# A three-network kernel: the feed-forwards' high weight tiles meet both input parts in one 512-column matmul

## The chip, the cores and the metric

One Trainium2 chip, one of its cores. The metric is the device time of one execution in microseconds (us). TensorE (PE) does the matmuls, VectorE (DVE) and ScalarE (ACT) the elementwise work, GpSimd (POOL) a few sums, SyncE (SP) issues the weight loads.

## The reference

Three networks run one after the other on 256 tokens of width 1024: two layers of feed-forward, attention mixer, feed-forward; two layers of feed-forward, convolution or stick-breaking attention, feed-forward; then two layers of attention and an expert lookup. The eight feed-forwards are what the change touches. Each computes

```python
def _rmsnorm(x, g):
    y = x32 * lax.rsqrt(jnp.mean(x32 * x32, axis=-1, keepdims=True) + RMS_EPS)
    return y * g
def _swiglu(x, w_gate, w_up, w_down):
    return (jax.nn.silu(x @ w_gate) * (x @ w_up)) @ w_down
x = x + 0.5 * _swiglu(_rmsnorm(x, g), w_gate, w_up, w_down)   # D_FF = 2816
```

## The kernel before

Everything lies transposed: a tile has 128 features as partitions and the 256 tokens as columns (T = 256), so x is 8 such tiles (DC = 8) and the hidden layer 22 (FC = 22). Matmuls are in fp32r, and to keep fp32 accuracy every operand is split into a high part (rounded) and a low part (the rest). One product of a 128x128 weight tile with a 128x256 input tile is then three matmuls, in `product`: high weights by high input (L655), high weights by low input (L656), low weights by high input (L657). The two input parts of a tile lie next to each other in memory (`h[:, c, 0]` and `h[:, c, 1]`, 256 columns each).

Weights come as slabs of 1 MB (128 x 2048). SyncE loads them into a ring of four (RING = 4). For each slab ScalarE makes the high part (`round_slab`, L1427, one of three buffers), VectorE the low part in place (`rest_slab`, L1916), and TensorE takes a slab when its low part is there (`take`). The order on each engine is the order in which the code is written; engines meet at semaphores, and an instruction that waits holds everything behind it on its engine.

A feed-forward is 33 slabs. The first 22, one for each hidden tile f, hold gate and up weights: 16 products, into the two banks of one of four bank pairs in PSUM (the accumulator memory). The other 11 (r) hold the down weights of two hidden tiles each: again 16 products, into all eight banks. The norm is applied late. The slabs multiply x times the gain, and the factor 1/rms of each token (`rstd`) is multiplied in when a bank pair is read (L2015). At the start TensorE runs slabs 0 and 1 interleaved and then the sums of squares (L726, L727); from them VectorE makes the mean (L1937), ScalarE the root (L1451) and VectorE the reciprocal (L1939). In the fifth feed-forward, the folded one, this chain is longer (`two_roots`, L2338 to L2343, with two roots on ScalarE, L1495 and L1496), since the final norm of the first network is worked into it. After that VectorE and ScalarE go in ticks, one for each slab. A tick of VectorE:

```python
        for tick in range(FC + 2):
            if tick < FC and not (fold and tick == 1):
                self.rest_slab()
...
            if tick == 0 and not fold:
                self.inverse_root(v.rstd, k.sum_bank[:, 0:T], 1, D)
```

followed by the low part of a hidden tile (L2001), gate times up (L2008), and the read of the bank pair with `rstd` (L2015). In tick f `rest_slab` handles slab f + 2.

## Time and profile before

| | |
|---|---|
| time of three runs | 4002.98 us median (3999.48 to 4004.27) |
| span of the profiled execution, first to last instruction | 4004.4 us |
| PE busy | 3909.7 us, 98% of the span, 34150 matmuls |
| DVE busy | 2736.3 us, 68% |
| ACT busy | 1987.8 us, 50% |
| mean granted clock of TensorE | 0.991 |

The span is what the profile has of the profiled execution's own time; nothing around it is given separately. It lies 1.4 us above the median of the runs and 0.1 us above the longest of them. Matmuls are pipelined: one of 256 columns is shown with 276 ns, but the next starts long before it ends, so rates are read from starts, not from durations. A busy share says that an engine had work in flight, not that it ran at its peak.

### The profile page before, as it was taken

The numbers are of one execution on the slowest core, as the hardware profiler recorded it, in microseconds if no ns is written. First come the engines' busy times: TensorE is split into PE (matmuls) and PEld (weight loads), VectorE is DVE, ScalarE is ACT, GpSimd is POOL, SyncE is SP. The second block draws the span as 40 slices with busy tenths as digits, with TensorE's granted clock in tenths as the row PEclk, the third lists the DMA queues.
The fourth block names the chain that finished last, engine by engine and source line by source line (L and its number), as shares of the span: only waits on it lengthen the run. The fifth ranks groups of instructions, "written<-read, shape, count | busy, mean of one in ns | idle before, by whom it ended". The sixth has DMA issues, their size and how long they took to land.

```text
span 4004.4 us, 78708 instructions
## 1 busy us (share of the span) xinstructions
PE 3909.7 (98%) x34150; PEld 3793.3 (95%) x34150; DVE 2736.3 (68%) x4071; ACT 1987.8 (50%) x2620; POOL 212.2 (5%) x277
## 2 busy tenths in 40 slices
PE   8999999999999999999999999999999999999999
PEld 8979999889998999999997999999998899999999
DVE  6566665666655656567555799956756699974855
ACT  5445444454544545465435545754444544764443
POOL 0011000110002000010023000000000000000000
PEclk9999999999999999999998999999999999999999
DMA  6534555345555455534550455456654455455754
GB/s 237 192 115 151 192 190 190 133 148 195 181 194 182 160 199 184 195 133 173 191 204 34 159 194 181 177 199 233 229 196 153 158 177 193 175 182 202 265 199 158
DMA packets 114791, 720.78 MB, mean 180 GB/s; under 512 B 13328, under 2 KB 13664, under 8 KB 32784
## 3 DMA queue, kind: packets, MB, share of 16 engines
q1 hardware_dynamic: 90144, 652.25, 45.9%
q10 hardware_dynamic: 19200, 37.01, 2.5%
q0 software_dynamic: 5104, 26.49, 1.9%
q8 instruction: 270, 4.42, 0.4%
q14 instruction: 73, 0.60, 0.0%
HBM read 692.48 MB, written 23.22 MB: 179 GB/s over the span
## 4 chain that ended last, share of the span: by engine, by line
PE 87%; DVE 7%; ACT 4%; issue 1%; POOL 0%; DMA 0%; ACTq 0%; DVEq 0%; POOLq 0%
PE psum L655 26%; PE psum L657 26%; PE psum L656 26%; PE psum L1408 3%; DVE slab_low L1916 2%; ACT slab_high L1427 2%; DVE h_parts L2219 1%; PE psum L1065 1%; PE psum L1048 1%; PE psum L875 1%; PE psum L1078 1%; ACT room L1670 1%; DVE room L2248 0%; DVE room L2253 0%; PE psum L1349 0%
## 5 line engine op out<-in xcount | busy, mean ns | idle before, releaser
L1916 DVE TENSOR_TENSOR slab_low<-slab,slab_high 128x2048 fp32r<-128x2048 f32 x622 | 1423.2, 2289 | 738.8 <-ACT slab_high L1427 736.6
L655 PE MATMUL psum<-h_parts,slab_high 128*128 128x256 f32 x5632 | 1578.2, 280 | 28.9 <-DVE h_parts L2219 18.6
L1427 ACT ACTIVATE slab_high<-slab 128x2048 fp32r<-128x2048 f32 x622 | 1189.3, 1912 | 785.4 <-PE psum L657 721.1
L656 PE MATMUL psum<-h_parts,slab_high 128*128 128x256 f32 x5632 | 1556.5, 276 | 0.0
L657 PE MATMUL psum<-h_parts,slab_low 128*128 128x256 f32 x5632 | 1556.1, 276 | 0.0
L655 PEld LDWEIGHTS psum<-h_parts,slab_high 128*128 128x128 f32 x5632 | 1063.5, 189 | 48.8 <-issue 24.0
L655 PE MATMUL psum<-hidden_parts,slab_high 128*128 128x256 f32 x3840 | 1063.5, 277 | 11.4 <-DVE hidden_parts L2166 4.8
L656 PEld LDWEIGHTS psum<-h_parts,slab_high 128*128 128x128 f32 x5632 | 1063.5, 189 | 2.4 <-issue 2.2
L657 PEld LDWEIGHTS psum<-h_parts,slab_low 128*128 128x128 f32 x5632 | 1062.8, 189 | 0.0
L656 PE MATMUL psum<-hidden_parts,slab_high 128*128 128x256 f32 x3840 | 1058.0, 276 | 0.0
L657 PE MATMUL psum<-hidden_parts,slab_low 128*128 128x256 f32 x3840 | 1058.0, 276 | 0.0
L655 PEld LDWEIGHTS psum<-hidden_parts,slab_high 128*128 128x128 f32 x3840 | 722.0, 188 | 21.6 <-issue 12.9
L656 PEld LDWEIGHTS psum<-hidden_parts,slab_high 128*128 128x128 f32 x3840 | 722.2, 188 | 0.0
L657 PEld LDWEIGHTS psum<-hidden_parts,slab_low 128*128 128x128 f32 x3840 | 722.0, 188 | 0.0
L1889 ACT ACTIVATE hidden_parts<-room 128x512 fp32r<-128x512 f32 x128 | 80.9, 632 | 303.7 <-PE psum L657 294.7
L1880 ACT ACTIVATE room<-psum 128x512 f32<-128x512 f32 x128 | 76.5, 598 | 283.1 <-PE psum L657 283.1
L2598 DVE TENSOR_TENSOR hidden_parts<-room,hidden_parts 128x512 fp32r<-128x512 f32 x128 | 88.2, 690 | 135.1 <-ACT hidden_parts L1889 134.9
L2015 DVE TENSOR_TENSOR room<-psum,room 128x512 f32<-128x512 f32 x176 | 121.3, 689 | 62.8 <-PE psum L657 61.7
L2569 DVE TENSOR_SCALAR room<-consts,room 128x128 f32<-128x128 f32 x512 | 136.4, 339 | 0.0
L1408 PE MATMUL psum<-room 128*128 128x128 f32 x1024 | 124.5, 275 | 0.0
L1670 ACT ACTIVATE room<-room 128x128 f32<-128x128 f32 (+1 forms) x160 | 71.4, 448 | 105.6 <-DVE room L2253 78.6
L1408 PEld LDWEIGHTS psum<-room 128*128 128x128 f32 x1024 | 119.4, 191 | 0.0
(346 smaller groups left out, 3326.0 us busy)
## 6 DMA issues: line engine op xcount, KB each, us to landing
slab<-in_up SPq DMA_DIRECT2D x176, 1024.0 KB, 4.8
slab<-in_keys_up SPq DMA_DIRECT2D x128, 1024.0 KB, 4.8
slab<-in_keys_down SPq DMA_DIRECT2D x128, 1024.0 KB, 4.8
slab<-in_down SPq DMA_DIRECT2D x88, 1024.0 KB, 4.8
slab<-in_w_in SPq DMA_DIRECT2D x16, 1024.0 KB, 4.8
slab<-in_wq SPq DMA_DIRECT2D x16, 1024.0 KB, 4.8
peer_gates<-room ACTq DMA_DIRECT2D x64, 256.0 KB, 2.3
room<-peer_gates ACTq DMA_DIRECT2D x64, 256.0 KB, 5.4
```

What stands on the lines that cost most here:

```text
L655: nc.tensor.matmul(out, lhs[0], rhs[0], start=first, stop=False, **options)
L656: nc.tensor.matmul(out, lhs[0], rhs[1], start=False, stop=False, **options)
L657: return nc.tensor.matmul(out, lhs[1], rhs[0], start=False, stop=last, **options)
L1408: mm = nc.tensor.matmul(bank[:, t, :], v.firsts[:, b % 2, t, :], v.seconds[b % 2][:, t, :], start=True, stop=True)
L1427: nc.scalar.activation(k.high[m % PARTS][:, 0:width], k.slabs[m % RING][:, 0:width], ACT.Copy).then_inc(k.rounded.up())
L1670: ex = nc.scalar.activation(row, row, ACT.Exp, bias=small[:, e:e + 1], accum_out=small[:, 4 + e:5 + e])
L1880: nc.scalar.activation(v.hidden[:, at:at + 2, :], k.banks[4 + r % 2].rearrange("p (e t) -> p e t", e=2), ACT.Gelu_apprx_tanh).then_inc(k.a ...
L1889: nc.scalar.activation(k.hidden[:, at:at + 2, 0, :], v.hidden[:, place:place + 2, :], ACT.Copy).then_inc(k.hidden_rounded.up())
L1916: nc.vector.tensor_tensor(k.low[m % RING][:, 0:width], k.slabs[m % RING][:, 0:width], k.high[m % PARTS][:, 0:width], ALU.subtract).then_in ...
L2015: nc.vector.tensor_tensor(both, k.bank_pairs[(f + k.first_pair) % 4][:, :, 0:T], v.rstd.unsqueeze(1).to_broadcast([P, 2, T]), ALU.mult).th ...
L2569: hot = nc.vector.tensor_scalar(v.seconds[b % 2][:, t, :], iota, v.slots[:, 1, t0 + t:t0 + t + 1], v.slots[:, 2, t0 + t:t0 + t + 1], ALU.i ...
L2598: nc.vector.tensor_tensor(k.hidden[:, at:at + 2, 1, :], v.hidden[:, place:place + 2, :], k.hidden[:, at:at + 2, 0, :], ALU.subtract).then_ ...
```

## The change

In the feed-forwards a product is now two matmuls: the high weights meet both input parts as one 512-column operand, which fills a whole bank, and the low weights add high input to the first half of it. The sum of both halves is taken later. For a gate/up slab ScalarE copies the second halves out of PSUM into a new buffer `second`, VectorE adds them to the first halves (`halves_added`), and the multiplication by `rstd` now reads the sum from memory. The first nine down slabs (WHOLE = 9) go the same way; VectorE adds their second halves to x (four instructions), while the last two down slabs keep the three-matmul product and write into the first halves alone. In the first place of a tick ScalarE now copies, and rounds the slab after that; the order of the rest of the tick changes too, and in the start of a feed-forward the roots now stand ahead of the first tick. The core of the diff:

```diff
+WHOLE = FC // 2 - 2
...
+    def product_apart(self, bank, lhs, both, first, last, **options):
+        nc = self.k.nc
+        nc.tensor.matmul(bank, lhs[0], both.rearrange("p a t -> p (a t)"), start=first, stop=False, **options)
+        return nc.tensor.matmul(bank[:, 0:T], lhs[1], both[:, 0], start=False, stop=last, **options)
...
# TensorE.ffn
-                nc.tensor.wait_ge(k.up_scaled.sem, k.up_scaled.at(f - 3))
+                nc.tensor.wait_ge(k.halves_added.sem, k.halves_added.at(f - 3))
...
-            if r == FC // 2 - 1:
-                nc.tensor.wait_ge(k.hidden_ready.sem, k.hidden_ready.at(FC))
+            if r >= WHOLE:
+                last = r == FC // 2 - 1
+                nc.tensor.wait_ge(k.hidden_ready.sem, k.hidden_ready.at(2 * r + 2))
                 for j, e, c in itertools.product(range(DC // 2), range(2), range(2)):
+                    if e == 0 and c == 0 and (last and j < 2 or not last and j == 2):
+                        nc.tensor.wait_ge(k.second_taken.sem, k.second_taken.at(3 + j if last else 2))
...
# ScalarE.ffn
+        else:
+            self.round_slab()
+            self.root(v.rstd)
         for tick in range(FC + 2):
-            if (2 if fold else 0) <= tick < FC:
+            if tick < FC:
+                f = tick
+                nc.scalar.wait_ge(k.slab_done.sem, k.slab_done.at(f + 1))
+                if f >= 2:
+                    nc.scalar.wait_ge(k.halves_added.sem, k.halves_added.at(f - 1))
+                nc.scalar.activation(v.second[:, f % 2], k.bank_pairs[(f + k.first_pair) % 4][:, :, T:2 * T], ACT.Copy).then_inc(k.second_copied.up())
                 self.round_slab()
-            if tick == 0 and not fold:
-                self.root(v.rstd)
...
-        for r in range(FC // 2):
+        for r in range(1, FC // 2):
             self.round_slab()
# VectorE.ffn
+        else:
+            self.inverse_root(v.rstd, k.sum_bank[:, 0:T], 1, D)
         for tick in range(FC + 2):
-            if tick < FC and not (fold and tick == 1):
+            both = v.both[:, tick % 2]
+            if tick < FC:
+                f = tick
+                nc.vector.wait_ge(k.second_copied.sem, k.second_copied.at(f + 1))
+                if f >= 2:
+                    nc.vector.wait_ge(k.multiplied.sem, k.multiplied.at(f - 1))
+                nc.vector.tensor_tensor(both, k.bank_pairs[(f + k.first_pair) % 4][:, :, 0:T], v.second[:, f % 2], ALU.add).then_inc(k.halves_added.up())
                 self.rest_slab()
-            if tick == 0 and not fold:
-                self.inverse_root(v.rstd, k.sum_bank[:, 0:T], 1, D)
...
+            if tick < FC:
+                nc.vector.wait_ge(k.halves_added.sem, k.halves_added.at(f + 1))
+                nc.vector.tensor_tensor(both, both, v.rstd.unsqueeze(1).to_broadcast([P, 2, T]), ALU.mult).then_inc(k.up_scaled.up())
...
-        for r in range(FC // 2 - 1):
+        for r in range(2, FC // 2):
             self.rest_slab()
+        nc.vector.wait_ge(k.slab_done.sem, k.slab_done.at(FC + WHOLE))
+        for n, j in enumerate((3, 2, 0, 1)):
+            halves = k.x[:, 2 * j:2 * j + 2, :]
+            if n >= 2:
+                nc.vector.wait_ge(k.pair_free.sem, k.pair_free.at(j + 1))
+            nc.vector.scalar_tensor_tensor(out=halves, in0=k.bank_pairs[j][:, :, T:2 * T], scalar=0.5, in1=halves,
+                                           op0=ALU.mult, op1=ALU.add).then_inc(k.second_taken.up())
+        nc.vector.wait_ge(k.second_taken.sem, k.second_taken.at(4))
+        self.rest_slab()
         self.owed = True
```

VectorE at the start of the first feed-forward, before. `slab_low_55` is the low part of slab 2, the third slab; L1937 and L1939 are the mean and the reciprocal, L2015 the read of the first bank pair.

```order
L2219 SCALAR_TENSOR_TENSOR h_parts<-x,vectors,h_parts 128x256 [waits h_rounded] x2
L1916 TENSOR_TENSOR slab_low_55<-slab_51,slab_high_59 128x2048 [waits slab_rounded]
L1937 TENSOR_SCALAR room<-psum 128x256 [waits squares_summed]
L1939 RECIPROCAL room<-room 128x256 [waits root_ready]
L2015 TENSOR_TENSOR room<-psum,room 128x512 [waits slab_done,dve_step]
```

The same place in the changed kernel (L1935 is `rest_slab`, L1956 the mean, L1958 the reciprocal, L2009 the sum of the two halves, L2023 the multiplication by `rstd`):

```order
L2247 SCALAR_TENSOR_TENSOR h_parts<-x,vectors,h_parts 128x256 [waits h_rounded] x2
L1956 TENSOR_SCALAR room<-psum 128x256 [waits squares_summed]
L1958 RECIPROCAL room<-room 128x256 [waits root_ready]
L2009 TENSOR_TENSOR room<-psum,room 128x512 [waits second_copied,dve_step]
L1935 TENSOR_TENSOR slab_low_55<-slab_51,slab_high_59 128x2048 [waits slab_rounded]
L2018 MEMSET room 1x16
L2023 TENSOR_TENSOR room<-room 128x512 [waits halves_added]
```

The low part of slab 2 stood ahead of the mean and now stands behind the mean, the reciprocal and the sum of the first halves. TensorE at the same place in the changed kernel (L736 and L737 are the sums of squares, then slab 2 begins):

```order
L736 MATMUL psum<-room,consts 128x256 [waits pool_move,squares_added]
L737 MATMUL psum<-room,consts 128x256
L666 MATMUL psum<-h_parts,slab_high_59 128x512 [waits small_load,slab_rest]
L667 MATMUL psum<-h_parts,slab_low_55 128x256
```

Behind the sums nothing stands on TensorE but slab 2, whose first matmul waits for `slab_rest`, that is for the low part just named; this order is the same as before, with two matmuls for three in a product.

## Rows read from the trace of the kernel before

**Rows 1.** The page, parts 1 and 4: busy time; the chain that ended last.

```profile
PE 3909.7 (98%) x34150; PEld 3793.3 (95%) x34150; DVE 2736.3 (68%) x4071; ACT 1987.8 (50%) x2620; POOL 212.2 (5%) x277
...
PE 87%; DVE 7%; ACT 4%; issue 1%; POOL 0%; DMA 0%; ACTq 0%; DVEq 0%; POOLq 0%
```

**Rows 2.** The page, part 5: busy us, mean ns | idle before, its releaser.

```profile
L1880 ACT ACTIVATE room<-psum 128x512 f32<-128x512 f32 x128 | 76.5, 598 | 283.1 <-PE psum L657 283.1
...
L2015 DVE TENSOR_TENSOR room<-psum,room 128x512 f32<-128x512 f32 x176 | 121.3, 689 | 62.8 <-PE psum L657 61.7
```

**Rows 3.** Timeline of PE, first feed-forward: start us, duration us, instruction.

```profile
59.95 0.28 PE L655 MATMUL psum<-h_parts,slab_high 128*128 128x256 f32 x1
...
79.67 0.28 PE L655 MATMUL psum<-h_parts,slab_high 128*128 128x256 f32 x1
```

**Rows 4.** Timeline of PE, sums of the last stage, 16 instructions in one row.

```profile
3992.60 3.61 PE L677 MATMUL psum<-room,consts 128*128 128x256 f32 x16
```

**Rows 5.** Instructions of line L677: duration in ns, min/median/max.

```profile
L677 PE MATMUL psum<-room,consts x16: 377/379/379, 3992.6 to 3995.8; 128*128 128x256 f32 x16
```

**Rows 6.** Timeline of PE, a later stage, 16 matmuls of 128 columns.

```profile
2501.94 1.95 PE L1408 MATMUL psum<-room 128*128 128x128 f32 x16
```

**Rows 7.** Timeline of VectorE at the start of the second feed-forward.

```profile
352.72 2.28 DVE L1916 TENSOR_TENSOR slab_low<-slab,slab_high 128x2048 fp32r<-128x2048 f32 x1
358.21 0.42 DVE L1937 TENSOR_SCALAR room<-psum 128x256 f32<-128x256 f32 x1 [3.22 <-PE psum L727]
359.12 1.75 DVE L1939 RECIPROCAL room<-room 128x256 f32<-128x256 f32 x1 [0.48 <-ACT room L1451]
360.91 0.69 DVE L2015 TENSOR_TENSOR room<-psum,room 128x512 f32<-128x512 f32 x1
361.52 2.28 DVE L1916 TENSOR_TENSOR slab_low<-slab,slab_high 128x2048 fp32r<-128x2048 f32 x1
...
367.53 0.68 DVE L2015 TENSOR_TENSOR room<-psum,room 128x512 f32<-128x512 f32 x1
...
371.00 0.68 DVE L2015 TENSOR_TENSOR room<-psum,room 128x512 f32<-128x512 f32 x1
```

**Rows 8.** Timeline of PE there: the third slab begins.

```profile
357.82 0.47 PE L655 MATMUL psum<-h_parts,slab_high 128*128 128x256 f32 x1
358.13 0.28 PE L656 MATMUL psum<-h_parts,slab_high 128*128 128x256 f32 x1
```

**Rows 9.** Timeline of VectorE near the start of the folded feed-forward.

```profile
1052.52 0.42 DVE L2343 TENSOR_TENSOR room<-room 128x256 f32<-128x256 f32 x1
...
1057.28 2.29 DVE L1916 TENSOR_TENSOR slab_low<-slab,slab_high 128x2048 fp32r<-128x2048 f32 x1 [0.78 <-ACT slab_high L1427]
```

**Rows 10.** Timeline of ScalarE there.

```profile
1053.30 0.40 ACT L1496 ACTIVATE room<-room 128x256 f32<-128x256 f32 x1
```

**Rows 11.** Timeline of PE there.

```profile
1047.61 0.28 PE L656 MATMUL psum<-h_parts,slab_high 128*128 128x256 f32 x1
...
1058.53 0.28 PE L657 MATMUL psum<-h_parts,slab_low 128*128 128x256 f32 x1
1059.62 0.39 PE L655 MATMUL psum<-h_parts,slab_high 128*128 128x256 f32 x1 [0.82 <-DVE slab_low L1916]
1059.85 0.28 PE L656 MATMUL psum<-h_parts,slab_high 128*128 128x256 f32 x1
```

**Rows 12.** Timeline of PE after its longest wait past the start.

```profile
1307.12 0.55 PE L655 MATMUL psum<-hidden_parts,slab_high 128*128 128x256 f32 x1 [4.84 <-DVE hidden_parts L2166]
```

**Rows 13.** Window behind that wait: PE busy (x instructions), granted clock, DMA.

```profile
1307.00:1312.00 5.00, 4.88 (x23) 0.50 0.00 0
```

**Rows 14.** Timeline of VectorE, steady stretch of the second feed-forward.

```profile
385.97 0.69 DVE L2015 TENSOR_TENSOR room<-psum,room 128x512 f32<-128x512 f32 x1 [0.46 <-PE psum L657]
```

**Rows 15.** Timeline of ScalarE: a usual round, and a slab that arrived late.

```profile
62.58 1.92 ACT L1427 ACTIVATE slab_high<-slab 128x2048 fp32r<-128x2048 f32 x1 [2.91 <-PE psum L657]
...
71.72 1.92 ACT L1427 ACTIVATE slab_high<-slab 128x2048 fp32r<-128x2048 f32 x1 [6.60 <-DMA slab<-in_up]
```

More of the change, by code:

```diff
@@ L232, in __init__ @@
         self.pair_done = signal("pair_done")
+        self.second_copied, self.halves_added = signal("second_copied"), signal("halves_added")
+        self.second_taken = signal("second_taken")
+        self.pair_free = signal("pair_free")
         self.hidden_rounded, self.hidden_ready = signal("hidden_rounded"), signal("hidden_ready")
@@ L352, in ffn_views @@
     v.square, v.squares, v.rstd = k.carve(DC, T), k.carve(2, T), k.carve(T)
-    v.both, v.acts = k.carve(2, 2, T), k.carve(2, T)
+    v.both, v.acts, v.second = k.carve(2, 2, T), k.carve(2, T), k.carve(2, 2, T)
     if fold:
@@ L691, in ffn @@
             at = (f + k.first_pair) % 4
-            pair = k.bank_pairs[at][:, :, 0:T]
+            pair = k.bank_pairs[at]
             if f >= 4:
-                nc.tensor.wait_ge(k.up_scaled.sem, k.up_scaled.at(f - 3))
+                nc.tensor.wait_ge(k.halves_added.sem, k.halves_added.at(f - 3))
             elif f >= 2 or k.first_pair < 2:
@@ L703, in ffn @@
                 firsts, lag = [], FIRST_LAG if first else DC if k.before == "ffn" else 2
-                pairs = [k.bank_pairs[g + k.first_pair][:, :, 0:T] for g in range(2)]
+                pairs = [k.bank_pairs[g + k.first_pair] for g in range(2)]
                 for step in range(DC + lag):
@@ L714, in ffn @@
                         for a in range(2):
-                            mm = self.product(pairs[g][:, a], [part[:, a, c, :] for part in firsts[g]], (k.h[:, c, 0, :], k.h[:, c, 1, :]), c == 0, c == DC - 1)
+                            mm = self.product_apart(pairs[g][:, a], [part[:, a, c, :] for part in firsts[g]], k.h[:, c], c == 0, c == DC - 1)
                         if c == DC - 1:
@@ L720, in ffn @@
                     for c in range(DC):
-                        mm = self.product(pair[:, a], [part[:, a, c, :] for part in w], (k.h[:, c, 0, :], k.h[:, c, 1, :]), c == 0, c == DC - 1)
+                        mm = self.product_apart(pair[:, a], [part[:, a, c, :] for part in w], k.h[:, c], c == 0, c == DC - 1)
                 mm.then_inc(k.slab_done.up())
@@ L754, in ffn @@
                     if f == 0 and n % 2 == 0:
-                        nc.tensor.wait_ge(k.up_scaled.sem, k.up_scaled.at(FC - 3 + n // 2))
+                        nc.tensor.wait_ge(k.halves_added.sem, k.halves_added.at(FC - 3 + n // 2))
                     cols = slice(e * D + c * P, e * D + (c + 1) * P)
-                    mm = self.product(k.banks[c][:, 0:T], (high[:, cols], low[:, cols]), (k.hidden[:, f, 0, :], k.hidden[:, f, 1, :]),
-                                      f == 0, False)
+                    mm = self.product_apart(k.banks[c], (high[:, cols], low[:, cols]), k.hidden[:, f], f == 0, f == 2 * WHOLE - 1)
             mm.then_inc(k.slab_done.up())
@@ L1489, in ffn @@
                     square.then_inc(k.squared.up())
-        for tick in range(FC + 2):
-            if (2 if fold else 0) <= tick < FC:
-                self.round_slab()
-            if tick == 0 and fold:
-                nc.scalar.wait_ge(k.meaned.sem, k.meaned.at(1))
-                nc.scalar.activation(v.rstd, v.rstd, ACT.Sqrt)
-                nc.scalar.activation(v.root, v.root, ACT.Sqrt).then_inc(k.rooted.up())
-            if tick == 0 and not fold:
-                self.root(v.rstd)
-            if tick == 1 and first:
+        if fold:
+            nc.scalar.wait_ge(k.meaned.sem, k.meaned.at(1))
+            nc.scalar.activation(v.rstd, v.rstd, ACT.Sqrt)
+            nc.scalar.activation(v.root, v.root, ACT.Sqrt).then_inc(k.rooted.up())
+        else:
+            self.round_slab()
+            self.root(v.rstd)
+        for tick in range(FC + 2):
+            if tick < FC:
[4 more added lines that the diff above has]
+                nc.scalar.activation(v.second[:, f % 2], k.bank_pairs[(f + k.first_pair) % 4][:, :, T:2 * T], ACT.Copy).then_inc(k.second_copied.up())
+                self.round_slab()
+            if tick == 0 and first:
                 nc.scalar.dma_start(k.bias_views.table[0:32, :], k.dram["bias_table"]).then_inc(k.small.up(), 16)
-            if tick >= 2:
-                f = tick - 2
-                nc.scalar.wait_ge(k.multiplied.sem, k.multiplied.at(f + 1))
-                nc.scalar.activation(k.hidden[:, f, 0, :], v.acts[:, f % 2, :], ACT.Copy).then_inc(k.hidden_rounded.up())
             if 1 <= tick <= FC:
@@ L1509, in ffn @@
                 nc.scalar.activation(gate, gate, ACT.Silu).then_inc(k.gated.up())
-        for r in range(FC // 2):
+            if tick >= 2:
+                f = tick - 2
+                nc.scalar.wait_ge(k.multiplied.sem, k.multiplied.at(f + 1))
+                nc.scalar.activation(k.hidden[:, f, 0, :], v.acts[:, f % 2, :], ACT.Copy).then_inc(k.hidden_rounded.up())
+        for r in range(1, FC // 2):
             self.round_slab()
@@ L1992, in ffn @@
                 self.then(done)
-            if tick == 1 and first:
+            if tick == 0 and first:
                 nc.vector.memset(k.bias_views.table[32:33, :], MASKED).then_inc(k.table_filled.up())
```

36 lines of the change are left out of this document (14 added, 22 removed).

## Prediction

> **What bounds the kernel now.** I read the page first. TensorE is busy 98% of the span, and the chain that ended last is 87% PE [rows 1]. So work that VectorE or ScalarE gains is hidden unless TensorE waits for it, and a saving on TensorE counts nearly in full. The costliest groups are the products. The 0.28 us of one matmul is a latency, so the rate comes from starts: from 59.95 to 79.67 lie 58 products of three matmuls [rows 3], 19.72 / 58 = 340.0 ns for a product, 113.3 ns for a matmul of 256 columns. Then I read the places where a stage begins, since a change of order shows there: what stands between the sums of squares and the third slab on each engine [rows 7, 8].
>
> **What TensorE saves.** Per feed-forward 22 slabs of 16 products and nine of 16 become two matmuls: 31 x 16 = 496, times eight is 3968. The last two down slabs keep three. No row shows 512 columns in fp32r, so the price is bounded. The nearest row is a sum: an instruction of L677 has 379 ns [rows 5] where a matmul of a product with the same 256 columns has 0.28 us [rows 3], 0.10 us more, which is another 256 columns at 2.4 GHz (0.107 us). Sixteen of them take 3.61 us [rows 4], so they start (3.61 - 0.38) / 15 = 215 ns apart, weights reloaded each time. I take 215 for the wide matmul and leave 113 for the low one: 328.7 ns, a saving of 11.3 ns. The upper bound: matmuls of 128 columns still start (1.95 - 0.28) / 15 = 111 ns apart [rows 6], though they bring half the columns, so a reload floor lies there and the low matmul cannot fall below 111: saving 13.6 ns. The lower bound is two pitches of 113.3 for the wide one: nothing saved. Sum: 3968 x 11.3 = **-44.8 us**, between 0 and -54.
>
> The page "TensorE: Matmul & The Clock Gate" of the Trainium skill, section "Back-to-back issue gap", has two rules for this. A lone gap is columns / 2.4 + 2.5 ns: 215.8 ns for 512, and the sum would stay as it is. A sustained stream with weight loads is said to give 131 ns for 512 columns: the sum would be 3968 x 95.7 = 380 us. Rows 4 are such a stream at 512 columns' worth of time, and they show 215, so I go by the first.
>
> **What ScalarE and VectorE get.** Per gate/up slab one more copy of 128x512 out of PSUM (598 ns by L1880) and one more add of that size (689 ns by L2015) [rows 2]; the multiplication is no dearer. Between slabs TensorE gives them 16 x 0.329 = 5.26 us. When VectorE is behind and never waits, a tick takes 371.00 - 367.53 = 3.47 us [rows 7]; with the add some 0.6 more, 4.1. It may start 0.75 us after its slab ends (the copy, and 0.15 for signals, an estimate), and so ends before 4.9: within 5.26. In a steady tick it waits for TensorE now [rows 14]. The low part of slab f + 2 is made behind the add: 0.75, then 0.61 from the start of the one to that of the other and 2.29 [rows 7], done 3.7 us after slab f, 1.6 us before it is needed. These are hidden by TensorE; without that cover they would be 176 x 1.29 = 227 us. A slab that lands late holds ScalarE's next copy: the worst in the trace kept it idle for 6.60 us, 3.7 us past the 2.91 that it waits for TensorE when nothing is late [rows 15]; the copy, add and low part behind it (5.5 us) would end 9.2 us after that slab's end, against 10.5. Nothing.
>
> The four instructions that put the second halves on x (4 x 0.69 us) follow slab r = 8; the low part of the next stage's first slab follows them and ends some 6 us after r = 8, needed at 10.9. TensorE's waits for them come at 2.7 us and later, when 1.5 us have been needed. Uncovered it would be 22 us in all; I cost it at nothing.
>
> **What the moved roots cost.** This is the term that decides. Before, VectorE makes the low part of slab 2 at 352.72, ahead of the mean [rows 7], so TensorE goes straight from the sums to slab 2: its second matmul starts at 358.13, its stream thus at 358.02 [rows 8]. Now that low part stands behind the mean, the root, the reciprocal and the first add, all of which start from the sums; TensorE has nothing else to do. The old rows give the new times, for the same instructions stand there in the same order, and only the slab of the low part is another: mean at 358.21, reciprocal from 359.12 to 360.87, first read of PSUM at 360.91, low part 361.52 to 363.80 [rows 7]. ScalarE's copy fits beside the reciprocal of 1.75 us. From the end of a low part to the stream TensorE needs 0.17 us (1057.28 + 2.29 = 1059.57; second matmul at 1059.85, less 0.11) [rows 9, 11]. So slab 2 streams at 363.97 instead of 358.02: 5.95 us idle, in seven feed-forwards **+41.7**.
>
> The folded one: VectorE's chain ends at 1052.94 [rows 9], the second root at 1053.70 [rows 10], then copy 0.60, add 0.61 to the next start, low part 2.29, and 0.17 with signals of 0.05: stream at 1057.4, before at 1047.50 [rows 11], so 9.9 us. In return the later wait (1058.64 to 1059.74, rows of the same group) goes: **+8.8**.
>
> Late next is VectorE, by one tick: it makes slab 3 ready some 3.4 us after slab 2 begins to stream, and slab 2 takes 5.3. No second wait.
>
> **The clock.** After a wait of 4.84 us TensorE resumed at 1307.12 [rows 12], and for the next 5 us it shows 0.50 granted, the lower level of 1.2 GHz: 23 matmuls where 44 would stand [rows 13]; its clock had fallen inside the wait. An idle time of 6 us should do the same eight times. Each spell of 4.9 us at half rate loses 2.45: **+19.6**, between 0 (no fall) and 28 (spells of 7 us). Some eight products of each spell save nothing: +0.7.
>
> **Sum.** -44.8 + 41.7 + 8.8 + 19.6 + 0.7 = +26.0 us on the profiled 4004.4, which lies 1.4 above the runs' median 4002.98. From the median: **4029 us**, 0.65% slower.
>
> **Rivals.**
> *The wide matmul is worth nothing* (two pitches): for it speaks that 113.3 is more than 256 columns at 0.42 ns, so some of a pitch may belong to the column stream; against it the 215 of L677. Then +71: 4074 us.
> *The clock doesn't fall*: for it speaks only that TensorE is dense up to the wait, where rows 12 follow a sparse stretch. Then +5.7: 4009 us. That is near the edge of "same", since a measurement of this kernel can tell some 0.2% (8 us) from no change.
> *Faster*: a wide matmul is much cheaper than its columns. It decides from a saving of 70.8 / 3968 = 17.9 ns on, a wide matmul of 208 ns. If the reload of weights alone sets a matmul's pitch, whatever its width, the wide one takes 113.3 too: saving 113.3 ns, 450 us, 3624 us. For it speaks that 128 columns and 256 go at nearly one pitch, 111 and 113 [rows 3, 6]; against it L677 [rows 4]. The sustained figure of the page above is of this kind. A smaller saving decides only with the clock: at 13.6 ns and with no fall it is 4000 us, still the same.
> *VectorE becomes the bound in every tick*: if the add or the copy takes longer on these banks and the low part comes 0.5 us late in 20 ticks of eight feed-forwards, +80 more: 4109 us. It needs the 1.6 us of slack gone; nothing in the rows does that.
>
> **Chances.** Forecast as it stands, with savings and spells in their bounds (4012 to 4055): 0.70. Worth nothing: 0.11. Clock doesn't fall, alone or with the greater saving: 0.09. Faster: 0.06. VectorE as bound: 0.04. The range 4008 to 4070 leaves out the faster cases, VectorE's and most of "worth nothing". Slower by over 0.2% is the first, second and fourth cases and a fourth of the third: 0.87; same 0.07; faster 0.06.
>
> **What would show it.** Right: in each feed-forward TensorE idle for about 6 us after L737, ended by the low part of L1935, one of about 10 us in the folded one; the granted clock at half behind it for some 5 us; wide matmuls of about 380 ns, products 328 to 329 ns apart in steady stretches; no waits of TensorE at other slabs, at the down slabs' first banks (the fourth pair is read 1.6 us after its slab, needed after 2.0) or at the last two. Wrong: products 335 ns apart or more, idle times of 0 to 3 us there, a granted clock that stays at 1, or waits for `slab_low` in many ticks.

## The result and the profile after

| | before | after |
|---|---|---|
| time of four runs | 4003.03 us median (3999.48 to 4004.27) | 4124.56 us median (4123.93 to 4129.71) |
| ratio | | 1.0303 (1.0291 to 1.0315) |
| span of the profiled execution | 4004.4 us | 4122.6 us, 118.2 more |
| mean granted clock | 0.991 | 0.984 |

The change costs 3.0%; 4029 us was forecast, with a range to 4070. The page after, parts 1 and 4 (busy time; the chain that ended last), answers to [rows 1]:

```profile
PE 3977.3 (96%) x30182; PEld 3672.8 (89%) x30182; DVE 2849.6 (69%) x4279; ACT 2069.5 (50%) x2796; POOL 213.4 (5%) x277
...
PE 87%; DVE 7%; ACT 3%; issue 2%; DMA 0%; POOL 0%; ACTq 0%; DVEq 0%
```

The 3968 matmuls fewer are there (34150 to 30182), and TensorE is still the bound. Yet it is busy for 68 us more. Part 5 of the page has the wide matmul (L666), and the timeline of TensorE, in a steady stretch of the second feed-forward, the rate (start us, duration us; it answers to [rows 3]):

```profile
L666 PE MATMUL psum<-h_parts,slab_high 128*128 128x512 f32 x2816 | 1017.3, 404 | 73.7 <-issue 26.8
```

```profile
409.45 0.40 PE L666 MATMUL psum<-h_parts,slab_high 128*128 128x512 f32 x1
...
411.22 0.40 PE L666 MATMUL psum<-h_parts,slab_high 128*128 128x512 f32 x1
411.45 0.28 PE L667 MATMUL psum<-h_parts,slab_low 128*128 128x256 f32 x1
411.57 0.40 PE L666 MATMUL psum<-h_parts,slab_high 128*128 128x512 f32 x1
...
415.81 0.40 PE L666 MATMUL psum<-h_parts,slab_high 128*128 128x512 f32 x1
```

From 409.45 to 415.81 lie 18 products: 353.3 ns each, where three narrow matmuls took 340.0. The wide one takes 233 to 236 ns to the next start, not 215; the low one behind it 117 to 120, not 113.

The waits of TensorE (line waited for: us in total, times, longest) show the moved roots:

```profile
PE psum L666 <- issue: 26.8, 4, 9.6
PE psum L666 <- DVE slab_low L1935: 26.1, 7, 5.7
...
PE psum L666 <- DVE room L2066: 4.6, 1, 4.6
```

"issue" holds the folded feed-forward's 9.62 us and three of the other seven stalls, which the trace puts under no releaser; the other four are in the second row. All seven last 5.67 to 5.72 us. The second feed-forward on VectorE (it answers to [rows 7]) and on TensorE:

```profile
377.44 0.42 DVE L1956 TENSOR_SCALAR room<-psum 128x256 f32<-128x256 f32 x1 [5.83 <-PE psum L737]
378.35 1.75 DVE L1958 RECIPROCAL room<-room 128x256 f32<-128x256 f32 x1 [0.48 <-ACT room L1465]
380.14 0.69 DVE L2009 TENSOR_TENSOR room<-psum,room 128x512 f32<-128x512 f32 x1
380.75 2.28 DVE L1935 TENSOR_TENSOR slab_low<-slab,slab_high 128x2048 fp32r<-128x2048 f32 x1
```

```profile
383.08 0.79 PE L666 MATMUL psum<-h_parts,slab_high 128*128 128x512 f32 x1 [5.67 <-DVE slab_low L1935]
...
383.89 0.63 PE L666 MATMUL psum<-h_parts,slab_high 128*128 128x512 f32 x1
...
384.53 0.63 PE L666 MATMUL psum<-h_parts,slab_high 128*128 128x512 f32 x1
```

That is the chain that the prediction drew, with its durations. Behind it the clock is at its lower level, 1.2 GHz. The windows are the first 5.87 us of that stream and 5.70 us a little later (from:to, length, PE busy (x instructions), granted clock, DMA share and GB/s; compare [rows 13]):

```profile
383.08:388.95 5.87, 5.87 (x18) 0.51 0.00 0
389.30:395.00 5.70, 5.70 (x35) 1.00 0.39 135
```

Last, a stall at a place where none was forecast: slab 7 of the first feed-forward. VectorE, then TensorE:

```profile
65.96 0.69 DVE L2009 TENSOR_TENSOR room<-psum,room 128x512 f32<-128x512 f32 x1 [3.06 <-ACT room L1516]
66.57 2.28 DVE L1935 TENSOR_TENSOR slab_low<-slab,slab_high 128x2048 fp32r<-128x2048 f32 x1
68.77 0.54 DVE L2065 COPY room<-psum 8x384 f32<-8x384 f32 x1
69.23 0.54 DVE L2066 COPY room<-psum 8x384 f32<-8x384 f32 x1
```

```profile
69.92 0.77 PE L666 MATMUL psum<-h_parts,slab_high 128*128 128x512 f32 x1 [4.62 <-DVE room L2066]
```

The two copies free the banks that slab 7 accumulates in. They stand in tick 6 of VectorE, now behind the sum of slab 6's halves (L2009), which exists only when slab 6 is done; TensorE waits for them at slab 7 and so has nothing to do between its end and theirs. Before, they waited for nothing of slab 6 and ended while TensorE worked on it, 1.6 us before slab 7 began at 56.89:

```profile
54.22 0.54 DVE L2037 COPY room<-psum 8x384 f32<-8x384 f32 x1
54.69 0.54 DVE L2038 COPY room<-psum 8x384 f32<-8x384 f32 x1
```

### The profile page after: what moved, and what is told of

Its sections match the earlier page's. It is cut to its first block, busy times and chain, and to the rows that moved or that the text cites. A ratio compares the mean times of both kernels' runs of the same rounds, so it can differ in the third digit from the quotient of the medians.

```text
span 4122.6 us, 71324 instructions
## 1 busy us (share of the span) xinstructions
PE 3977.3 (96%) x30182; PEld 3672.8 (89%) x30182; DVE 2849.6 (69%) x4279; ACT 2069.5 (50%) x2796; POOL 213.4 (5%) x277
## 4 chain that ended last, share of the span: by engine, by line
PE 87%; DVE 7%; ACT 3%; issue 2%; DMA 0%; POOL 0%; ACTq 0%; DVEq 0%
PE psum L666 23%; PE psum L659 15%; PE psum L661 15%; PE psum L660 15%; PE psum L667 11%; PE psum L1422 3%; DVE slab_low L1935 2%; ACT slab_high L1441 1%; DVE h_parts L2247 1%; PE psum L1079 1%; PE psum L1062 1%; PE psum L889 1%; PE psum L1092 1%; ACT room L1689 1%; DVE room L2276 0%
## 5 line engine op out<-in xcount | busy, mean ns | idle before, releaser
L1935 DVE TENSOR_TENSOR slab_low<-slab,slab_high 128x2048 fp32r<-128x2048 f32 x622 | 1421.0, 2287 | 517.3 <-ACT slab_high L1441 514.8
L666 PE MATMUL psum<-h_parts,slab_high 128*128 128x512 f32 x2816 | 1017.3, 404 | 73.7 <-issue 26.8
L659 PE MATMUL psum<-h_parts,slab_high 128*128 128x256 f32 x2816 | 796.2, 283 | 7.4 <-DVE slab_low L1935 4.7
L667 PE MATMUL psum<-h_parts,slab_low 128*128 128x256 f32 x2816 | 801.0, 284 | 0.0
L660 PE MATMUL psum<-h_parts,slab_high 128*128 128x256 f32 x2816 | 778.8, 277 | 0.0
L661 PE MATMUL psum<-h_parts,slab_low 128*128 128x256 f32 x2816 | 778.5, 276 | 0.0
L659 PE MATMUL psum<-hidden_parts,slab_high 128*128 128x256 f32 x2688 | 747.8, 278 | 11.4 <-DVE hidden_parts L2194 4.8
L660 PE MATMUL psum<-hidden_parts,slab_high 128*128 128x256 f32 x2688 | 742.2, 276 | 0.0
L666 PEld LDWEIGHTS psum<-h_parts,slab_high 128*128 128x128 f32 x2816 | 538.9, 191 | 213.0 <-issue 47.4
L659 PEld LDWEIGHTS psum<-h_parts,slab_high 128*128 128x128 f32 x2816 | 531.8, 189 | 22.6 <-issue 10.8
L660 PEld LDWEIGHTS psum<-h_parts,slab_high 128*128 128x128 f32 x2816 | 531.9, 189 | 2.2 <-issue 2.2
L659 PEld LDWEIGHTS psum<-hidden_parts,slab_high 128*128 128x128 f32 x2688 | 506.7, 189 | 22.0 <-issue 12.9
L660 PEld LDWEIGHTS psum<-hidden_parts,slab_high 128*128 128x128 f32 x2688 | 506.9, 189 | 0.0
L661 PEld LDWEIGHTS psum<-hidden_parts,slab_low 128*128 128x128 f32 x2688 | 506.7, 189 | 0.0
L666 PE MATMUL psum<-hidden_parts,slab_high 128*128 128x512 f32 x1152 | 407.4, 397 | 0.0
L1516 ACT ACTIVATE room<-psum 128x512 f32<-128x512 f32 x176 | 105.2, 598 | 458.2 <-PE psum L667 458.2
L2009 DVE TENSOR_TENSOR room<-psum,room 128x512 f32<-128x512 f32 x176 | 121.6, 691 | 266.9 <-ACT room L1516 266.7
```

The source lines that it names most:

```text
L659: nc.tensor.matmul(out, lhs[0], rhs[0], start=first, stop=False, **options)
L660: nc.tensor.matmul(out, lhs[0], rhs[1], start=False, stop=False, **options)
L661: return nc.tensor.matmul(out, lhs[1], rhs[0], start=False, stop=last, **options)
L666: nc.tensor.matmul(bank, lhs[0], both.rearrange("p a t -> p (a t)"), start=first, stop=False, **options)
L667: return nc.tensor.matmul(bank[:, 0:T], lhs[1], both[:, 0], start=False, stop=last, **options)
L1516: nc.scalar.activation(v.second[:, f % 2], k.bank_pairs[(f + k.first_pair) % 4][:, :, T:2 * T], ACT.Copy).then_inc(k.second_copied.up())
```

## The experiments

Twelve kernels ran: two that divide the change, two that vary how wide matmuls follow one another, six that vary the operand's place or the width, and two probes. "Wide" is a matmul of 512 columns, "narrow" one of 256. Times from here on are of one run each, beside the kernel before on the same chip, except in a1_start and a2_roots_only; so they serve to place a kernel, and prices are read from starts in the traces.

**The start repaired (a1_start).** The low part of slab 2 goes ahead of the roots again, the bias copies ahead of the sum; the wide matmuls stay.

```diff
# VectorE.ffn of the changed kernel
+        self.rest_slab()
         if fold:
             self.two_roots(v, k.sum_bank[:, 0:T], k.sum_bank[:, T:2 * T])
...
         for tick in range(FC + 2):
             both = v.both[:, tick % 2]
+            if tick == 6 and first:
+                self.bias_lines()
...
-                self.rest_slab()
+                if f != 1:
+                    self.rest_slab()
...
-            if tick == 6 and first:
-                self.bias_lines()
```

> The changed kernel with the low part of slab 2 made ahead of the roots again (and the two bias copies of the first feed-forward at the head of their tick). Theory 1, the slowdown is idle time of TensorE at the starts plus its clock plus a wide matmul dearer than two narrow ones: the eight idle times (49 us), the one of 4.6 us and the spells at half clock behind them (some 20 us) go, while products stay at 353 ns: 4045 to 4056 us. Rival, the clock falls because products of two matmuls are less dense, not because of the idle times: the spells stay, 4065 to 4075 us.

Measured: 4062.47 us (4053.28 to 4065.77, four runs) beside 4005.4 (seven runs), ratio 1.0136 (1.0119 to 1.0153); 4063.1 us span. TensorE goes straight from the sums to slab 2:

```profile
366.31 0.59 PE L737 MATMUL psum<-room,consts 128*128 128x256 f32 x2
366.56 0.58 PE L666 MATMUL psum<-h_parts,slab_high 128*128 128x512 f32 x1
366.98 0.28 PE L667 MATMUL psum<-h_parts,slab_low 128*128 128x256 f32 x1
...
479.97 0.28 PE L667 MATMUL psum<-h_parts,slab_low 128*128 128x256 f32 x1
```

The seven stalls, the one at slab 7 and the clock's falls behind them are gone: in the 5 us behind the sums the granted clock is 1.00 seven times, where the changed kernel had 0.50 to 0.71. So it was the idle time that brought the clock down, and not products of two matmuls, the rival of this expectation. The folded feed-forward keeps a stall of 5.05 us, now at slab 3, with 0.61 behind it; its stretch is 6.8 us longer than the others (120.19 for 113.42). The expectation left that out and came out 6 us too low. About 62 us of the 121, give or take 7, come from the moved roots and copies. The rest is in the products, which need no stall to be slow: this stretch, slabs 2 to 21, ends at 479.97 with the start of its last matmul, 113.41 us. In the kernel before it is 109.44, from 357.82 [rows 8] to 467.26:

```profile
467.26 0.28 PE L657 MATMUL psum<-h_parts,slab_low 128*128 128x256 f32 x1
```

That is 3.97 us for 320 products, 12.4 ns each: the 13.3 between two steady products (353.3 and 340.0), less a short wait at slab 3 that the kernel before has in each feed-forward (0.20 us idle at 363.85) and this one has not. 3968 x 12.4 = 49.2 us and the 6.8 make 56 of the measured 57.1 us over the kernel before.

**The roots alone (a2_roots_only).** The kernel before with its three matmuls; only slab 2's low part is moved behind the roots and the first read.

```diff
# VectorE.ffn of the kernel before
-            if tick < FC and not (fold and tick == 1):
+            if 1 <= tick < FC:
                 self.rest_slab()
             if tick == 0 and fold:
-                self.rest_slab()
                 self.two_roots(v, k.sum_bank[:, 0:T], k.sum_bank[:, T:2 * T])
...
+            if tick == 0:
+                self.rest_slab()
```

> The kernel before, with three matmuls to a product, and only the order at the start of a feed-forward changed: the low part of slab 2 stands behind the roots and the first read. Theory 1: seven idle times of 5.7 us, one of 9 to 10, and eight spells at half clock of about 2.4 us lost each, 4065 to 4076 us. Rival, the idle times matter only because of the new copies and adds: 4003 to 4030 us.

Measured: 4067.03 us (4063.63 to 4069.28, four runs), ratio 1.0151 (1.0134 to 1.0168). The stall of the second feed-forward in the timeline of TensorE:

```profile
373.30 0.58 PE L655 MATMUL psum<-h_parts,slab_high 128*128 128x256 f32 x1 [5.68 <-DVE slab_low L1916]
```

Seven such stalls of 5.68 to 5.72 us, 9.06 in the folded one, and a granted clock of 0.50 to 0.62 for 5 us behind each, as was expected of this run. The prediction's terms for idle time and clock, 41.7 + 8.8 + 19.6 = 70.1 us, measure 62 alone.

**Wide matmuls in a row, and wide ones only.** In a3_grouped the eight wide matmuls of a bank come first and its eight narrow ones behind; in a4_allwide the low weights too meet 512 columns, so that low by low is added, which the reference's products leave out.

```diff
# a3_grouped, gate and up slabs (down slabs alike)
-                    for c in range(DC):
-                        mm = self.product_apart(pair[:, a], [part[:, a, c, :] for part in w], k.h[:, c], c == 0, c == DC - 1)
+                    for c in range(DC):
+                        nc.tensor.matmul(pair[:, a], w[0][:, a, c, :], k.h[:, c].rearrange("p a t -> p (a t)"), start=c == 0, stop=False)
+                    for c in range(DC):
+                        mm = nc.tensor.matmul(pair[:, a, 0:T], w[1][:, a, c, :], k.h[:, c, 0], start=False, stop=c == DC - 1)
# a4_allwide, product_apart
-        return nc.tensor.matmul(bank[:, 0:T], lhs[1], both[:, 0], start=False, stop=last, **options)
+        return nc.tensor.matmul(bank, lhs[1], both.rearrange("p a t -> p (a t)"), start=False, stop=last, **options)
```

> The changed kernel with the matmuls of each eight products in another order: eight wide ones, then eight narrow ones. Theory A, the change of width from one matmul to the next costs: wide ones start 215 to 220 ns apart, narrow ones 113, a product 329 to 333 ns, some 4035 to 4050 us. Theory B, 512 columns in fp32r cost more by themselves: wide ones stay at 233 to 240 ns, narrow ones go back to 113, a product 346 to 353 ns, 4100 to 4125 us.

> The changed kernel with the low weights too meeting all 512 columns (the product of both low parts is added, which the three-matmul product leaves out), so that all matmuls of these products are wide. Theory A: 215 to 220 ns from start to start, a product 430 to 440 ns, 4430 to 4470 us. Theory B: 233 to 240 ns, a product 466 to 480 ns, 4570 to 4630 us.

Measured: a3_grouped 4113.99 us, a4_allwide 4546.69, one run each. The timeline of a3_grouped puts a group in a row:

```profile
62.11 2.01 PE L731 MATMUL psum<-h_parts,slab_high 128*128 128x512 f32 x8
63.95 1.10 PE L733 MATMUL psum<-h_parts,slab_low 128*128 128x256 f32 x8
```

Eight wide ones start within 63.95 - 62.11 = 1.84 us, 230 ns each; eight narrow ones (1.10 - 0.28) / 7 = 117. A stream of wide ones alone:

```profile
59.77 0.39 PE L666 MATMUL psum<-h_parts,slab_high 128*128 128x512 f32 x1
...
61.16 0.39 PE L666 MATMUL psum<-h_parts,slab_high 128*128 128x512 f32 x1
```

1.39 us for six, 232 ns (the starts follow in steps of 225, 231 and 237). So it isn't the alternation that makes 231 of 215: a wide matmul costs that among its like too, and some 3 ns of the 234 come of the alternation. The narrow ones take 117 in a group of eight as well. Theory A is out in both runs. Theory B is right about the wide ones but for their size, a little high, so that a4_allwide's time lies between the two ranges; the narrow ones don't go back to its 113.

**The place of the moving operand.** h_parts and hidden_parts begin 240 bytes past a multiple of 512 (RESIDUE). b1_before_residue0 is the kernel before with place 0; b2_wide_residue0 and b4_wide_residue128 are a1_start with 0 and 128.

```diff
-RESIDUE = 240
+RESIDUE = 0
```

> The kernel before with the input parts (h, early and hidden) 240 bytes earlier against a multiple of 512 bytes (RESIDUE 0 instead of 240). Theory C, a matmul's pitch is its columns times a rate of the moving operand's reads, which hangs on where it lies: narrow matmuls leave 113.3 ns for 116 to 121 and the time is 4080 to 4200 us. Theory F, a fixed overhead of a matmul: 113.3 ns stays, 3995 to 4012 us.

> The changed kernel with the start put right (a1_start) and RESIDUE 0. Theory C: the product moves away from 353 ns in step with what the kernel before shows at this place. Theory F: 353 ns and 4055 to 4066 us.

> a1_start with RESIDUE 128. Theory C: a product other than 353 ns, and if a place suits wide matmuls better, down to 340 (4005 to 4015 us); theory F: 353 ns, 4055 to 4066 us.

Measured: 4139.89, 4125.28 and 4142.59 us beside 4004.11. Two starts of L655 in b1_before_residue0, 56 products apart:

```profile
59.83 0.28 PE L655 MATMUL psum<-h_parts,slab_high 128*128 128x256 f32 x1
...
79.77 0.28 PE L655 MATMUL psum<-h_parts,slab_high 128*128 128x256 f32 x1
```

19.94 / 56 = 356.1 ns for three narrow matmuls, 118.7 each, in a kernel of which no order is changed: the 113.3 on which the prediction rests belongs to a place. By the records of the other two a wide product takes 351 ns on average at place 0 and at 128 (347.5 to 353.3 by feed-forward at 128). So the wide product doesn't follow the narrow ones, as theory C had it. Both whole times lie far over the 4055 to 4066 us named for an unchanged product, since RESIDUE moves the operands of all other stages too: their products of three narrow matmuls go from 340 to 356 and 360. At place 0 the change saves a little, 356 to 351 and 14.6 us between the two runs, in a kernel that is 136 us slower there.

**Fewer columns (b3_columns).** a1_start with 320 columns for 512 and 128 for 256 (but in a bank's first matmul); the products of the columns left out are missing.

```diff
-        nc.tensor.matmul(bank, lhs[0], both.rearrange("p a t -> p (a t)"), start=first, stop=False, **options)
-        return nc.tensor.matmul(bank[:, 0:T], lhs[1], both[:, 0], start=False, stop=last, **options)
+        wide = 2 * T if first else 320
+        nc.tensor.matmul(bank[:, 0:wide], lhs[0], both.rearrange("p a t -> p (a t)")[:, 0:wide], start=first, stop=False, **options)
+        return nc.tensor.matmul(bank[:, 0:128], lhs[1], both[:, 0, 0:128], start=False, stop=last, **options)
```

> a1_start with 320 instead of 512 columns in all wide matmuls but the first of a bank, and 128 instead of 256 in the narrow ones (part of the products is left out). Theory C: 320 columns start 142 to 148 ns before the next (0.443 to 0.46 ns a column), 128 columns stay at the weight floor of 111 to 114. Theory F (columns at 2.4 GHz and 20 ns for a wide matmul): 320 columns 153 ns or more. Slabs become as short as a tick of VectorE, so the time may be set by that; the pitch inside slabs is what counts.

Measured: 3763.15 us; by its records a product takes 260 ns from start to start. The recorded starts within a product (some 200 ns, then 60) don't divide it in a way that prices either matmul; 260 less the 111 of a stream of 128 columns in d1_probe, below, would leave 149 for 320. That stretch of d1_probe measures 320 columns directly.

**A place for each feed-forward.** The gate/up slabs' input begins at 240, 224, 232, 236, 208, 176, 112 and 48 in the eight feed-forwards, in the kernel before (c1_places_before) and in a1_start (c2_places_wide).

```diff
...
+        lead = 60
+        if stage == "ffn":
+            lead = (60, 56, 58, 59, 52, 44, 28, 12)[self.feeds]
+            self.feeds += 1
+        self.h = self.h_places[:, lead:lead + DC * 2 * T].rearrange("p (c a t) -> p c a t", a=2, t=T)
```

> The kernel before, three matmuls for a product; only the place of the feed-forward's input is changed, one place in each of the eight feed-forwards: it begins 240, 224, 232, 236, 208, 176, 112 and 48 bytes past a multiple of 512. The inputs of all other stages and the hidden layer stay at 240. Theory 'place': a narrow matmul starts 113 to 114 ns after the one ahead in the first feed-forward's gate and up slabs, and some 118 to 120 ns (as at place 0) in those of most of the others; with some six of eight feed-forwards at 118 to 120, 6 x 22 x 16 x 3 x 5.5 ns = 35 us are added: 4025 to 4050 us. Theory 'stream' (an even stream of matmuls of one width has 113 ns wherever its input lies, place 0 having disturbed something else): 113 to 114 in all eight, 4000 to 4010 us.

> The changed kernel with the low part of slab 2 ahead of the roots again, as in a1_start, and the same eight places of the input in the eight feed-forwards. Theory 'place and columns': a product of a wide and a narrow matmul stays between 346 and 356 ns at every place, since a wide one costs 231 to 236 and the narrow one 114 to 120, and no place brings the two below the 340 of three narrow matmuls at place 240; time 4055 to 4080 us. Rival 'a place of its own': the wide operand has a good place as the narrow one has at 240, and there a product takes 328 to 338 ns, the 215 and 113 of the forecast; a kernel with that place would then be faster than before.

Measured: 4051.66 and 4070.14 us beside 4004.91. Mean ns from a start to the next of its kind, worked out from the records of each feed-forward:

```
place                     240  224  232  236  208  176  112   48
three narrow (c1)         340  361  361  361  360  356  353  359
wide and narrow (c2)      354  351  392  347  354  351  354  351
```

The first expectation held, with all seven others slow instead of some six: 113 in the first feed-forward, 117 to 122 in the others, so an even stream alone doesn't make the 113; it takes the place. The place alone doesn't make it either: in a3_grouped eight narrow ones in a row, at that same place, take 117. The second held but for place 232, which at 392 lies beyond its 356; no place came under 340.

**All places, other engines idle (d1_probe).** Behind the last stage of the kernel before, TensorE runs groups of seven products at 128 places, and streams of one width.

```diff
# TensorE.norm_stage
+        def meet(part, at, width, c, shift=0):
+            n = next(turn)
+            weights = part[n % 2][:, c * P + shift:(c + 1) * P + shift]
+            nc.tensor.matmul(k.banks[free[n // 32 % len(free)]][:, 0:width], weights, k.h_all[:, at + c * 2 * T:at + c * 2 * T + width], start=True, stop=True)
...
+        for place in range(128):
+            narrow(LEAD + place)
+        for place in range(128):
+            wide(LEAD + place)
+        for shift in range(16):
+            wide(LEAD, 4 * shift)
+        for width in (512, 448, 384, 320, 288, 256, 224, 192, 160, 128):
+            for _ in range(3):
+                for c in range(DC - 1):
+                    meet(k.high, LEAD, width, c)
...
```

> The kernel before with matmuls added behind its last stage, while all other engines are idle; their results are not used. On TensorE, with weights in turn from the high and low slabs and a moving operand from the feed-forwards' input buffer, in groups of seven products: (1) three narrow matmuls for a product, the operand beginning at each of 128 places 4 bytes apart from 240 on; (2) a wide and a narrow matmul at the same 128 places; (3) the same at place 240 with the weights shifted by 0 to 240 bytes; (4) streams of one width, 512 down to 128 columns, 21 each. Theory 'place and columns': the narrow triples take 339 to 341 ns at some places and 350 to 366 at others; the wide products take 345 to 395, under 340 nowhere; a stream of one width has about 0.44 to 0.46 ns for a column (231 ns at 512, 144 at 320) down to a floor of about 111. Rival 'a place of its own': at some places a wide product takes 328 to 338 ns. Rival 'other engines': with all of them idle a wide product at place 240 takes 328 to 338 instead of 353, since their traffic had slowed it. The added time, about 1100 us, is of no interest.

Measured, mean ns of a product (the last six of seven), by the operand's place in bytes; behind 256 bytes the numbers repeat within 5 ns:

```
place      three narrow, places +0 +4 ... +28     wide and narrow
240        340 365 365 359 360 371 366 353        353 356 360 347 351 355 353 347
272 (16)   340 362 362 353 356 363 360 359        347 357 354 347 347 352 347 349
304 (48)   358 360 361 356 341 364 361 357        350 358 352 344 352 357 353 347
336 (80)   357 360 361 353 354 363 363 352        354 360 357 347 353 353 352 343
368 (112)  360 367 360 353 359 370 360 352        353 362 350 353 348 361 353 346
400 (144)  356 366 360 352 349 363 358 353        348 347 357 344 347 358 347 347
432 (176)  355 361 360 353 340 353 363 352        351 352 353 343 352 358 356 344
464 (208)  360 366 360 360 360 362 362 358        353 358 350 346 351 356 353 346
```

At 240 the narrow triple is at its best, 340, which four of 64 places come to (within 1 ns); the wide product there is 353, as in the full kernel, though every other engine is idle. So their traffic isn't the cause. The best wide product is 343, not under 340, as theory 'place and columns' had it; the narrow ones reach 371, over its 366. The streams of one width, in the timeline a row for each:

```profile
4697.13 4.55 PE L693 MATMUL psum<-h_parts,slab_high 128*128 128x512 f32 x19
...
4701.75 4.30 PE L693 MATMUL psum<-h_parts,slab_high 128*128 128x448 f32 x20
...
4709.89 2.81 PE L693 MATMUL psum<-h_parts,slab_high 128*128 128x320 f32 x18
...
4725.15 1.95 PE L693 MATMUL psum<-h_parts,slab_high 128*128 128x128 f32 x16
```

Span less one duration (0.39, 0.37, 0.31 and 0.28 us), over the count less one: 231, 207, 147 and 111 ns. At 2.4 GHz the columns alone are 213, 187, 133 and 53: with a weight load for each matmul a wide one pays 14 to 20 ns over its columns. In every run each matmul has a weight load of its own, so whether the load makes these 14 to 20 isn't shown. Under 256 columns there is a floor: the starts of 224, 192 and 160 give 111 to 112 too. Those of 256 begin with seven at 114 to 121 and go on at 113 to 114, so the narrow price of the kernel before needs narrow ones ahead of it besides the place. For 128 weight columns the Trainium skill ("TensorE: Matmul & The Clock Gate", section "LDWEIGHTS (loading the stationary operand)") has a load time of columns / 1.2, 107 ns by its figure; the floor of 111 is 4 ns over that. That the load sets the floor isn't shown, since these streams all load 128 columns.

**Both places at once (d2_joint).** Since the weights' place alone (the third loop above) moved the wide product between 347 and 359, all pairs of 64 places of the operand and 16 of the weights, 4 bytes apart, were run, five products each.

```diff
...
+        for shift in range(16):
+            for place in range(64):
+                wide(LEAD + place, shift)
```

> The kernel before with matmuls added behind its last stage, all other engines idle, results not used: products of a wide and a narrow matmul in groups of five, for each of 64 places of the moving operand (4 bytes apart, over 256 bytes, after which the pattern of d1_probe repeats) with each of 16 places of the weights (4 bytes apart). In d1_probe either place alone moved the product between 343 and 362 ns. Theory 'place and columns': no pair of places brings it under 338 ns, since the 512 columns need 225 at least and the narrow one 113; the best is 338 to 343. Rival 'a pair of places': some pair takes 326 to 337; with the input parts and the weight slabs laid so, the change would gain 3968 times what is saved of 340, and that version will be run.

Measured: 1024 pairs between 342.75 and 393.5 ns, mean 352.0; 23 are under 344, none under 342. In those 23 a wide matmul takes 227 to 228 on average and a narrow one 115 to 116. The pair (232, weights unshifted) has 393, the 392 of the third feed-forward of c2_places_wide on another chip; in d1_probe the same pair had 353, so what ran ahead of it counts too. At none of these pairs does the changed product come under the 340 that the kernel before has. At the best it would still lose 3 ns, 3968 x 3 = 12 us as an estimate, so no version was run at it. These are groups of five, and place 232 shows that a group and a long stream can differ (353 in d1_probe, 392 in c2_places_wide); that no layout goes under 340 in a whole kernel is likely by these numbers, but not shown.

## Why the prediction was wrong

**What failed: the price of the wide matmul ("What TensorE saves").** The step took 215 ns from L677 [rows 4, 5] and 113 for the low one, 328.7 against 340.0. Measured are 233 to 236 and 117 to 120, 353.3. The term of -44.8 us is +49 (12.4 x 3968, by a1_start's stretch). Three things were wrong in it.

First, the rows were of another type. L677 isn't an fp32r product: its tiles (`consts` and the squares) are declared fp32, which the rows print as f32 like the others, and its weights are the same constant each time; that its 256 columns take what 512 would at 2.4 GHz was an arithmetic that happened to fit. The trace of the kernel before could have shown it: L837 is a matmul of fp32 tiles with 512 columns, and two of them in a row start 1.02 - 0.59 = 0.43 us apart, twice the 215 of 256. In the timeline, and in the source view (duration in ns, min/median/max):

```profile
250.40 1.02 PE L837 MATMUL psum<-room,consts 128*128 128x512 f32 x2
```

```profile
L837 PE MATMUL psum<-room,consts x16: 590/618/1223, 226.2 to 250.8; 128*128 128x512 f32 x16
```

The 128 columns of L1408 [rows 6] are fp32 as well. From 111 to 215 to 429 ns every further column costs 0.81 to 0.84, so the 111 needs no reload floor to explain it. That fp32r has a floor, at the same 111, is shown only by d1_probe: the prediction had that number right by luck.

Second, the 113.3 was taken for the price of a narrow matmul; it is the best case of a place (b1, c1, d1), and next to a wide matmul that case is lost. Third, the bound, "between 0 and -54", let two pitches of 113.3 be the worst: nothing in the rows says that a wide matmul can't cost more than two narrow ones, and it does, 231 against 227. The bound left out a loss, and with it the range. Of the rivals, "worth nothing" (4074) points the right way and stops at the same wall; "VectorE becomes the bound" (4109) is nearer in time by chance, for TensorE waits for no `slab_low` in steady ticks.

The Trainium skill ("TensorE: Matmul & The Clock Gate", section "Back-to-back issue gap") has two rules, which give 215.8 and 131 ns for 512 columns; here 231 to 236 were measured, so the first is 15 to 20 too low for this stream and the second far off.

**The moved roots: right.** 5.67 to 5.72 us idle seven times for 5.95, together 39.9 for 41.7; the folded one 9.62 for 9.9 and, less the later wait (0.82 us idle [rows 11]), which is gone, 8.8 as forecast. Reading the new stall out of the old rows, with only the order exchanged, worked to 0.3 us.

**The clock: right, a little large.** It falls at every such stall: in the 5 us behind the nine the granted clock is 0.50 to 0.71. Less the idle time, the stretches of the eight feed-forwards are 0.9 to 2.4 us longer than an undisturbed one of a1_start, 12.7 in all, and 2.5 more is lost behind the stall at slab 7: 15.2 for 19.6. At the lower level a product takes 640 ns (384.53 - 383.89), less than twice 353; the forecast had reckoned with twice. The part of a spell in which TensorE runs was 2.9 to 6.2 us, where the forecast had 4.9.

**"No waits at other slabs": wrong once.** Slab 7 of the first feed-forward, 4.6 us. The order of VectorE's instructions in that tick was in the code; the prediction went through what the new add delays for `slab_low`, and not through the copies that share tick 6.

**ScalarE and VectorE: right.** In steady ticks VectorE waits for ScalarE's copy, which waits for TensorE, and has 1.5 us to spare; before it waited for TensorE directly, 0.46 us [rows 14]:

```profile
397.92 0.69 DVE L2009 TENSOR_TENSOR room<-psum,room 128x512 f32<-128x512 f32 x1 [1.49 <-ACT room L1516]
```

**The sum.** 49.2 + 39.9 + 8.8 + 4.6 + 15.2 = 117.7 us, against 118.2 of the two spans. That it closes to 0.5 us can be partly luck: outside these nine spells the lower clock holds for 76 us in the trace before and 66 in the one after, which the sum leaves out.

## What to carry to other kernels

A matmul rate belongs to a stream: the widths that alternate, a weight load for each, and where the operands lie. Before trading instructions for columns, time both forms in a stream like the kernel's own, and take no price from a row of another type; the price of two narrow matmuls is no upper bound for a wide one. When an instruction is put at the head of a tick, list all that stood behind that point in the tick, one-off work too, and ask who waits for each. When the low part that the next slab needs moves behind a chain of roots, the old rows give the stall; here, with stalls of 4.6 us and more, a fall of the clock came on top each time.

## What the runs showed of the hardware

The start-to-start time of fp32r matmuls depends on where the moving operand begins, in steps of 4 bytes with a period of 256: 340 to 371 ns for three matmuls of 256 columns. The weights' place counts as well (347 to 359 at one place of the operand). So does what ran ahead: 353 and 393 for the same pair of places, and 118 for the first seven narrow ones of a stream that then goes at 113. Idle engines change nothing at place 240: 353 both ways. With a new weight tile each time, 128 to 224 columns of fp32r cost the same 111 to 112 ns, and 512 cost 231; of fp32, 256 cost 215 and 512 cost 429. Why 512 columns take 18 ns over their 213 and what in the memory's layout makes a good place was not found out: the runs vary place and width from outside, and no row of a trace shows the reads.
